# Output product, memory's keys and values, and cross attention: from an order written by hand to one stream placed by durations

## The reference, cut to what matters

```python
x = x + jnp.concatenate([attn_out, mlstm_out], axis=-1) @ w_out[l]
x = x + cross_attention(rmsnorm(x, norm_xattn_g[l]), rmsnorm(mem, norm_mem_g[l]),
                        wq_x[l], wkv_x[l], wo_x[l])
hf = rmsnorm(x, norm_ffn_g[l])          # the feed-forward part follows

def cross_attention(hq, hm, wq, wkv, wo):   # mem has 256 rows; 4 heads of 256
    q = (hq @ wq).reshape(B, S, X_HEADS, X_HEAD_DIM)
    kv = hm @ wkv
    ...
    s = jnp.einsum('bshd,bmhd->bhsm', q, k) * (X_HEAD_DIM ** -0.5)
    a = jax.nn.softmax(s, axis=-1)
    o = jnp.einsum('bhsm,bmhd->bshd', a, v).reshape(B, S, X_HEADS * X_HEAD_DIM)
    return o @ wo
```

## Time and profile before

| | |
|---|---|
| median of 3 runs | 2723.42 us (2719.78 to 2723.84) |
| the profiled execution | 2715.8 us, of which the span from first to last instruction is 2714.0 |
| TensorE busy (matmuls) | 2475.5 us, 91% of the span |
| VectorE, ScalarE busy | 1424.6 us (52%), 942.4 us (35%) |
| mean granted TensorE clock | 0.953 of full speed |
| the stretch that is changed | 500.36 to 926.5 us |

### The profile page before, as it was taken

How to read it: one execution, slowest core, us unless ns; L and a number is a source line. 1 busy time by engine, 2 the same in 40 slices (tenths; PEclk the granted TensorE clock), 3 DMA queues, 4 the chain that set the end, 5 groups by cost and what they waited for, 6 DMA issues and landing times.

```text
span 2714.0 us, 41559 instructions
## 1 busy us (share of the span) xinstructions
PE 2475.5 (91%) x18010; PEld 1991.9 (73%) x18010; DVE 1424.6 (52%) x2500; ACT 942.4 (35%) x1584; POOL 79.6 (3%) x61
## 2 busy tenths in 40 slices
PE   3989988988899999999999998799999999589879
PEld 2777765777778788888888886566777777377757
DVE  4633855565234655534555446653354455666653
ACT  4324542344223333322333324543322232234341
POOL 0000000000000000000000000020000001200000
PEclk9999997989999999999999999888999998699989
DMA  4444310334211333333333333322222311211033
GB/s 144 111 123 123 104 48 1 122 95 131 63 55 52 91 99 94 100 93 101 94 98 96 95 93 107 106 74 87 93 61 66 114 47 35 89 39 39 10 121 120
DMA packets 358335, 233.07 MB, mean 86 GB/s; under 512 B 9604, under 2 KB 332292, under 8 KB 358024
## 3 DMA queue, kind: packets, MB, share of 16 engines
q1 hardware_dynamic: 355416, 224.83, 27.7%
q10 hardware_dynamic: 2736, 5.57, 0.5%
HBM read 211.50 MB, written 18.87 MB: 85 GB/s over the span
## 4 chain that ended last, share of the span: by engine, by line
PE 80%; DVE 11%; ACT 5%; issue 1%; DMA 1%; SPq 0%; DVEq 0%; ACTq 0%
PE PS L1239 19%; PE PS L1240 18%; PE PS L1241 18%; PE PS L1583 4%; PE PS L1225 3%; PE PS L1259 2%; PE PS L1261 2%; PE PS L1260 2%; PE PS L1501 1%; DVE SR L1713 1%; DVE SB L1839 1%; ACT SR L2332 1%; PE PS L1467 1%; PE PS L1431 1%; PE PS L1521 1%
## 5 line engine op out<-in xcount | busy, mean ns | idle before, releaser
L1239 PE MATMUL PS<-SR 128*128 128x512 f32 (+2 forms) x2384 | 959.9, 403 | 57.7 <-DVE SR L1713 40.4
L1240 PE MATMUL PS<-SR 128*128 128x512 f32 (+2 forms) x2384 | 935.5, 392 | 0.0
L1241 PE MATMUL PS<-SR 128*128 128x512 f32 (+2 forms) x2384 | 934.1, 392 | 0.0
L1713 DVE TENSOR_TENSOR SR<-SB,SR 128x1024 fp32r<-128x1024 f32 (+2 forms) x328 | 395.9, 1210 | 467.4 <-ACT SR L2332 467.1
L1239 PEld LDWEIGHTS PS<-SR 128*128 128x128 f32 (+1 forms) x2384 | 455.4, 191 | 182.4 <-DVE SR L1713 43.5
L1241 PEld LDWEIGHTS PS<-SR 128*128 128x128 f32 (+1 forms) x2384 | 455.1, 191 | 96.8
L1240 PEld LDWEIGHTS PS<-SR 128*128 128x128 f32 (+1 forms) x2384 | 456.0, 191 | 89.7 <-issue 2.2
L2332 ACT ACTIVATE SR<-SB 128x1024 fp32r<-128x1024 f32 (+2 forms) x328 | 338.3, 1036 | 295.1 <-DMA SB<-in_w_down 115.0
L1583 PEld LDWEIGHTS PS<-SB 64*64 64x64 f32 x4096 | 129.6, 137 | 41.0 <-issue 21.6
L1583 PE MATMUL PS<-SB 64*64 64x64 f32 x4096 | 142.4, 223 | 11.9 <-DVE SB L2213 5.5
L1225 PE MATMUL PS<-SB 128*128 128x128 f32 (+3 forms) x680 | 103.5, 288 | 41.6 <-DVE SB L2095 14.0
(11 more groups left out here) (238 smaller groups left out, 2502.4 us busy)
## 6 DMA issues: line engine op xcount, KB each, us to landing
SB<-in_w_in SPq DMA_DIRECT2D x110, 512.0 KB, 4.0
SB<-in_w_up SPq DMA_DIRECT2D x88, 512.0 KB, 3.9
SB<-in_w_out SPq DMA_DIRECT2D x32, 512.0 KB, 4.5
SB<-in_w_down SPq DMA_DIRECT2D x32, 512.0 KB, 4.2
SB<-in_w_ada SPq DMA_DIRECT2D x12, 1024.0 KB, 6.7
asides<-SB SPq DMA_DIRECT2D x40, 256.0 KB, 4.4
SB<-in_wkv SPq DMA_DIRECT2D x16, 512.0 KB, 3.8
SB<-in_wq SPq DMA_DIRECT2D x16, 512.0 KB, 4.2
```

Of the source, the lines that this page charges most:

```text
L1239: pe.matmul(out, whi[:, k - k0, :], hi[k], start=(k == 0), stop=False)
L1240: pe.matmul(out, whi[:, k - k0, :], lo[k], start=False, stop=False)
L1241: i = pe.matmul(out, wlo[:, k - k0, :], hi[k], start=False, stop=(k == j.K - 1))
L1713: v.tensor_tensor(m.f32r(a, kn * cn), m.f32(a, kn * cn), m.f32r(a + 1024, kn * cn).bitcast(F32), SUB).then_inc(*on("split.v", p))
```

## The change

The stretch is written by `flow`. `cross` yields its softmax as three steps (`cross_s`, `cross_x`, `cross_p`), waits for room and for the block ahead of it, and two streams take the eight blocks from one list. `mix_parts` becomes `mix_part(h, k)`; those of half 1 are a side stream (`mix_later`). The norms `mem`, `x0`, `x1` and `ffn0` are side streams, each from the point on at which its input is complete. `work` gets durations for the new steps. The pieces of `out0` shrink to four k-blocks, those of `q` and `o` to two. The scaling of the softmax is one instruction with a broadcast operand where it was four. x is read again in two transfers of 2 MB, one for each half, and memory's 1 MB stands between them in SP's queue; `mem_load` is gone. An addition into x waits for its own half alone.

```diff
             dst=lambda t, h=h: m.mo[:, t, hs(h)])
         job(f"out{h}", d["w_out"], 0, 128, 8, m.MX[h], lambda k, h=h: [("mix.v", "lo", h, k)], "add", "gemm.v",
-            cut=4 if h else 8, dst=lambda t, h=h: m.xs[h][t], wait=lambda t: [("x", 7)], half=h)
-        job(f"q{h}", d["wq"], 0, 128, 8, m.H2[h], normed(f"x{h}"), "copy", "gemm.a",
+            cut=4, dst=lambda t, h=h: m.xs[h][t], wait=lambda t, h=h: [(f"xr{h}", 0)], half=h)
+        job(f"q{h}", d["wq"], 0, 128, 8, m.H2[h], normed(f"x{h}"), "copy", "gemm.a", cut=2,
             dst=lambda t, h=h: m.qx[:, t, hs(h)], wait=UP("pe", "kv0"))
         job(f"o{h}", d["wo"], 0, 128, 8, m.H2[h], lambda k, h=h: [("cross.v", "lo", n) for n in range(4 * h, 4 * h + 4)],
-            "add", "gemm.v", dst=lambda t, h=h: m.xs[h][t], half=h,
+            "add", "gemm.v", cut=2, dst=lambda t, h=h: m.xs[h][t], half=h,
             wait=lambda t, h=h: [("gemm.v", "ev", f"out{h}", t)])
         job(f"ug{h}", d["w_up"], 0, 128, 22, m.HB, normed(f"ffn{h}"), "conv_f", "gemm.a", half=h,
             dst=lambda t: m.gf[t], wait=UP("pe", "down0" if h else "o1"))
...
+    if name[:6] == "cross_":
+        return {"cross_s": [("pe", 3.5), ("v", 1.6)], "cross_x": [("a", 2.0)], "cross_p": [("v", 1.6)],
+                "cross_t": [("pe", 0.9), ("a", 0.6), ("v", 0.3)], "cross_o": [("pe", 3.6), ("a", 1.1), ("v", 1.25)]}[name]
+    if name == "mix_part":
+        return [("a", 0.6), ("v", 0.7)]
     if name[:3] == "ml_":
         return {"ml_e": [("pe", 1.7), ("v", 2.8)], "ml_x": [("a", 1.5)], "ml_q": [("pe", 1.7), ("v", 1.4)],
                 "ml_s": [("pe", 1.75), ("v", 1.22)], "ml_k": [("pe", 0.9), ("a", 3.1)], "ml_o": [("pe", 0.9), ("v", 1.22)],
...
     def cross(self, n):
+        if n:
+            yield from self.after(("cs", n - 1))
+        yield from self.after("kv", f"q{n // 4}")
+        yield from self.room((self.pairs, 1), (self.P, 1))
+        self.done.add(("cs", n))
         b, free = self.pairs.take()
         p, pfree = self.P.take()
         st = self.stat()
+        yield [("cross_s", n, b, free, st)]
         self.pairs.give(b, ("cross.a", "x", n))
-        yield [("cross_s", n, b, free, p, pfree, st)]
+        yield [("cross_x", n, b, p, pfree, st)]
+        yield [("cross_p", n, p, st)]
+        if n:
+            yield from self.after(("ct", n - 1))
+        yield from self.room((self.pairs, 1), (self.PT, 1))
+        self.done.add(("ct", n))
         b, free = self.pairs.take()
         self.P.give(p, ("cross.pe", "t", n))
         q, qfree = self.PT.take()
         self.pairs.give(b, ("cross.a", "pt", n), ("cross.v", "pt", n))
         yield [("cross_t", n, b, free, p, q, qfree)]
+        yield from self.room((self.pairs, 1))
         b, free = self.pairs.take()
         self.PT.give(q, ("cross.pe", "o", n))
         self.pairs.give(b, ("cross.v", "lo", n))
-        return [("cross_o", n, b, free, q)]
+        yield [("cross_o", n, b, free, q)]
+        self.done.add(("cross", n))
+
+    def crosses(self, units):
+        while units:
+            yield from self.cross(units.pop(0))
+
+    def mix_later(self):
+        for k in range(0, 8, 2):
+            yield [("mix_part", 1, k), ("mix_part", 1, k + 1)]
+        self.done.add("parts")
+        yield [("mark", "parts")]
+
+    def memory(self):
+
+        yield from self.gemmT("kx")
+        for c in range(2):
+            yield from self.gemmN(f"vx{c}")
+        yield [("mark", "kv")]
+        kv = ("upto", "pe", "kv")
+        for i in range(2):
+            self.P.give(i, kv)
+            self.PT.give(i, kv)
+        self.done.add("kv")
 
     def ffn(self, half):
         for t in range(23):
@@ -1162,27 +1202,17 @@
                   self.gates(), self.gate_logs(), self.ada(), self.rms("mix1", self.room), *[self.windows(units) for _ in range(3)], self.attended(),
                   self.mlstm(0, 2), self.mlstm(1, 3))
         self.mark("ml")
-        self.emit(("x_again",), ("mix_parts", 0), ("mix_parts", 1))
-        self.mark("parts")
-        self.run(T("out0"))
-        self.emit(("mem_load",))
-        self.together(T("out1"), chain(self.rms("mem"), self.rms("x0")))
-        self.mark("kv0")
-        self.together(chain(T("kx"), N("vx0"), N("vx1")), self.rms("x1"))
-        self.mark("kv")
-        self.run(T("q0"))
-        self.mark("q0")
-        kv = ("upto", "pe", "kv")
+        self.emit(("x_again",), *[("mix_part", 0, k) for k in range(8)])
         self.P, self.PT = Places([]), Places([])
-        for i in range(2):
-            self.P.give(i, kv)
-            self.PT.give(i, kv)
-        self.together(T("q1"), staggered([self.cross(n) for n in range(4)], 2), 2)
-        self.mark("q1")
-        self.together(T("o0"), staggered([self.cross(n) for n in range(4, 8)], 2), 2)
-        self.mark("o0")
-        self.together(T("o1"), self.rms("ffn0"))
-        self.mark("o1")
+        units = list(range(8))
+        crossed = lambda h: self.after(*[("cross", n) for n in range(4 * h, 4 * h + 4)])
+        self.flow(chain(T("out0"), self.after("parts"), T("out1"), self.flagged("kv0", ("mark", "kv0")), self.after("mem"),
+                        self.memory(), self.after("x0"), T("q0"), self.flagged("q0", ("mark", "q0")), self.after("x1"), T("q1"),
+                        self.flagged("q1", ("mark", "q1")), crossed(0), T("o0"), self.flagged("o0", ("mark", "o0")), crossed(1),
+                        T("o1"), self.flagged("o1", ("mark", "o1"))),
+                  self.mix_later(), *[self.crosses(units) for _ in range(2)], self.rms("mem", self.room),
+                  chain(self.after("out0", "parts"), self.rms("x0", self.room)), chain(self.after("kv0"), self.rms("x1", self.room)),
+                  chain(self.after("o0"), self.rms("ffn0", self.room)))
         self.conv = 0
         self.run(self.ffn(0))
...
-    def mix_parts(h):
+    def mix_part(h, k):
         hi, lo = m.MX[h][0:2]
-        for k in range(8):
-            w.wait_ge(*at("mix.a", "hi", h, k))
-            v.tensor_tensor(lo[k], m.mixs[k][:, 512 * h:512 * h + 512], hi[k].bitcast(F32), SUB).then_inc(
-                *on("mix.v", "lo", h, k))
-
-    def cross_s(n, b, free, p, pfree, st):
-        P, s = v3(m.Pv2[p], 4), v3(pair(b), 4)
-        mx, nm, sm, _ = stats(st, 4)
+        w.wait_ge(*at("mix.a", "hi", h, k))
+        v.tensor_tensor(lo[k], m.mixs[k][:, 512 * h:512 * h + 512], hi[k].bitcast(F32), SUB).then_inc(*on("mix.v", "lo", h, k))
+
+    def cross_s(n, b, free, st):
+        mx, nm, _, _ = stats(st, 4)
         w.wait_ge(*at("cross.pe", "s", n))
-        for e in S.each(pfree):
-            w.wait_ge(*e)
-        v.tensor_reduce(mx, s, AX.X, MAX).then_inc(*on("cross.v", "max", n))
+        v.tensor_reduce(mx, v3(pair(b), 4), AX.X, MAX).then_inc(*on("cross.v", "max", n))
         w.wait_ge(*at("cross.v", "max", n))
         v.tensor_scalar(nm, mx, -1.0 / 16, None, MUL).then_inc(*on("cross.v", "neg", n))
+
+    def cross_p(n, p, st):
+        P, sm = v3(m.Pv2[p], 4), stats(st, 4)[2]
         w.wait_ge(*at("cross.a", "x", n))
         v.reciprocal(sm, sm).then_inc(*on("cross.v", "rcp", n))
         w.wait_ge(*at("cross.v", "rcp", n))
-        for g in range(4):
-            i = v.tensor_scalar(P[:, g, :], P[:, g, :], sm[:, g:g + 1], None, MUL)
-        i.then_inc(*on("cross.v", "p", n))
+        v.tensor_tensor(P, P, sm.unsqueeze(2).to_broadcast([128, 4, 256]), MUL).then_inc(*on("cross.v", "p", n))
 
     def cross_t(n, b, free, p, q, qfree):
...
 
-    def mix_parts(h):
+    def mix_part(h, k):
         for e in ("pe", "v", "a"):
             for x in S.upto(e, "ml"):
                 w.wait_ge(*x)
-        for k in range(8):
-            a.activation(m.MX[h][0][k], m.mixs[k][:, 512 * h:512 * h + 512], ACT.Copy).then_inc(*on("mix.a", "hi", h, k))
-
-    def cross_s(n, b, free, p, pfree, st):
+        a.activation(m.MX[h][0][k], m.mixs[k][:, 512 * h:512 * h + 512], ACT.Copy).then_inc(*on("mix.a", "hi", h, k))
+
+    def cross_x(n, b, p, pfree, st):
         P, s = v3(m.Pv2[p], 4), v3(pair(b), 4)
         mx, nm, sm, _ = stats(st, 4)
         w.wait_ge(*at("cross.v", "neg", n))
+        for e in S.each(pfree):
+            w.wait_ge(*e)
         for g in range(4):
             i = a.activation(P[:, g, :], s[:, g, :], ACT.Exp, bias=nm[:, g:g + 1], scale=1.0 / 16, accum_out=sm[:, g:g + 1])
...
         mlstm_done()
-        for k in range(8):
-            sp.dma_start(m.XT[:, k, :], d["xT"][k * 128:(k + 1) * 128, :]).then_inc(*on("x", k, by=16))
-
-    def mem_load():
-        mlstm_done()
-        sp.dma_start(v3(m.work(28672, 2048), 8), d["memT"].rearrange("(k p) n -> p k n", p=128)).then_inc(
-            *on("mem", 0, by=16))
+        for h in range(2):
+            sp.dma_start(m.XT[:, :, 512 * h:512 * h + 512],
+                         d["xT"][:, 512 * h:512 * h + 512].rearrange("(k p) n -> p k n", p=128)).then_inc(*on(f"xr{h}", 0, by=16))
+            if not h:
```

(2 more changed lines are left out.)

10 lines of the change are left out of this document (5 added, 5 removed).

## The result

The changed kernel takes **2681.08 us** (median of four runs, 2676.67 to 2685.52) against 2721.60 for the kernel before beside it (2719.35 to 2723.84, four runs). The ratio is 0.9857, 95% interval 0.984 to 0.9875: 1.4% faster. The forecast was 2685. The profiled execution took 2676.67 (span 2674.8).

What follows compares the result with a forecast made beforehand. TensorE's waits and low clock from `out0` to `o1` were taken as the bound. Of 55.7 us lost, 17.5 would stay (5.9, 6.0, 5.6, 0), so 38.2 less: 2685 us, range 2675 to 2696.

Steps and rivals of the forecast that it cites:

- the 55.7 us that the change can give: TensorE's loss against full-clock work: 54.1 us from `out0` to `o1` plus 1.6 behind; the most the change can give.
- A: `out0` and `out1`: 5.9 of 11.3 us lost stays, as 1.4 cold start, 3.5 memory's transfer, 1.0 norm wait.
- Memory's transfer: Early `out0`: memory lands late, its squares delay a split, TensorE waits 2.6 us plus 0.9 of clock, 3.5 new.
- The norm `x0`: Moves into `out1`: sum 9.4 us behind the end of `out0`, waiting 1.0; its outputs lie under `out1`.
- B: Memory's keys and values (`kx`, `vx0`, `vx1`): 6.0 of 18.9 us lost stays, VectorE still the tightest of the stretch.
- C: `q0` to `o1` with cross attention: 5.6 of 23.9 us stays, 2.9 scaled from planned sliding-window stretch 208 to 388, 2.7 unnamed.
- The scaling: Cross attention's softmax: one instruction for four adds 0.8 us on VectorE over eight blocks, hidden under TensorE's work.
- Behind the stretch: First feed-forward tile after `o1`: its 1.6 us wait goes, leaving 0; the order of what follows is untouched.
- B did not keep its loss: Rival for memory's keys and values: VectorE can't follow the 2.86 us tiles, 12.9 of gain goes, 2698 us; chance 0.14.
- no transpose waited: Slower rival in cross attention: each of eight transposes meets its softmax unfinished, 65 us lost there, 2745 us; chance 0.04.
- Memory's norm did not block the front: Rival in `out0`: memory's squares, additions and sum hold the engines 11 to 14 us, not 3.5; 2694 us; chance 0.12.
- waits only change place: Rival over the stretch: TensorE stands at side steps instead, 50 of 55.7 us stay, 2718 us or more; chance 0.04.

Runs made afterwards that it cites:

- one_step: The kernel before, with one side step for each tile of `q1` and `o0` where there were two: 2697.85 us, ratio 0.9929 to the kernel before.
- whole_tiles: The changed kernel without the cut of `q` and `o` tiles into two pieces: 2691.84 us, ratio 0.9895 to the kernel before.
- prompt: The changed kernel with the planner booking nothing for weight splits in the stretch, so norms come promptly: 2680.96 us, ratio 0.9869 to the kernel before.
- outs: The changed kernel with a norm's output step booked on VectorE alone in the stretch: 2675.31 us, ratio 0.9832 to the kernel before.
- stream_c: The changed kernel with everything ahead of `q0` in the old hand order, new transfers kept: 2702.58 us, ratio 0.9943 to the kernel before.

## Why the prediction was right, step by step

- **What bounds it, and the 55.7 us that the change can give.** Right. The stretch got 39.1 us shorter and the median fell by 40.5, where 38.2 was forecast.
- **A, 5.9.** Measured 4.5, by other terms. The cold start, 1.4, is 3.0 in this execution, since the clock stays longer at the 1.2 GHz level. That is not the change: one_step has the order of the kernel before up to here, whole_tiles that of the changed kernel, and each start comes with both. The first 8 us of `out0`, in before and one_step, then in changed and whole_tiles (8 x (1 - 0.82) = 1.4 lost, 8 x (1 - 0.62) = 3.0):

```profile
500.36:508.36 8.00, 8.00 (x29) 6.54 (x30) 8.00 (x14) 7.89 (x15) 0.00 (x0) 0.82 0.92 330
497.15:505.15 8.00, 8.00 (x23) 6.32 (x24) 8.00 (x14) 7.88 (x15) 0.00 (x0) 0.62 0.95 347
```

```profile
497.54:505.54 8.00, 8.00 (x23) 6.32 (x24) 5.26 (x9) 3.81 (x8) 0.00 (x0) 0.62 0.99 346
497.65:505.65 8.00, 8.00 (x29) 6.54 (x30) 5.27 (x9) 3.82 (x8) 0.00 (x0) 0.82 0.99 347
```

  In all four TensorE waits 3.4 us just ahead. What decides between the two starts, these runs don't show.

- **Memory's transfer, 3.5.** The mechanism was right: the squares are the longest wait of ScalarE there, the split follows them, and TensorE waits at the third tile. The measured 1.28, with no clock lost, is smaller by the luck of the long start. Memory landed as forecast: the squares began 11.6 us behind the issue of x's first transfer at 496.41 (I had 11.2). But TensorE wanted the tile 1.7 us later, since it had run at the low clock for longer. In whole_tiles, with the same order and the short start that the prediction had assumed, the wait is 2.66 (I had 2.6), the clock reads 0.89 from 505 to 520, and A loses 6.1. The changed kernel, then whole_tiles:

```profile
507.99 2.57 ACT L2418 ACTIVATE SB<-SB 128x256 f32<-128x256 f32 x8 [6.64 <-DMA SB<-in_memT]
...
512.82 0.50 PE L1269 MATMUL PS<-SR 128*128 128x512 f32 x1 [1.28 <-DVE SR L1743]
```

```profile
512.83 0.50 PE L1269 MATMUL PS<-SR 128*128 128x512 f32 x1 [2.66 <-DVE SR L1743]
```

- **The norm `x0`, 1.0 of wait, sum 9.4 us behind `out0`, outputs under `out1`.** The failed step. The planner's table was read, and not that its running times only go forward; the sum came some 30 us later. That is why nothing waits for it. And the assumed placement would have cost more than its 1.0: in prompt that wait was 0.8, but memory's sum waited 3.3 us more and lowered the clock, for which the sum of A had nothing.
- **B, 6.0.** Mis-sized at 0.9 for the same reason. For the placement that it assumed the size was good: prompt lost 7.2. The reason was half right. The step of reciprocal and two outputs does make a split late (1.9 us in prompt, 2.8 in outs); the other wait comes from the squares in ScalarE's queue (2.2 in prompt, 1.1 in the changed kernel), which the prediction didn't count. VectorE's load was no bound: it is busy 29.8 us of 46.2.
- **C, 5.6.** Mis-sized at 9.4. The row of 208 to 388 was the right neighbour for the blocks themselves (forecast 2.9; stream_c and prompt lose 0.6 and 0.4), and there the 2.7 without a name went too. In one_step 3.0 without a name remain. What I left out is `x1`'s norm reaching into the first two blocks: 4.3 idle (3.60 and 0.72) and 3.0 at the low clock in the second scores. The rest, 2.1, has no row that I can name.
- **The scaling, 0.8 under cover.** Right: 1.22 against 1.14 a block, and no difference in time. The prediction says that by the figures of the Trainium skill, "VectorE: DVE Perf Modes", the sum is the same 0.8. That was reckoned wrong: four times 128 + 150 cycles against 1,024 + 150, at the page's 0.96 GHz, differ by 0.06 us a block, an estimate of 0.5 for the eight. That rate and fixed cost nearly cancel, the rows bear out.
- **Behind the stretch, 0.** Right for the feed-forward's first tile (4.47 busy of 4.47). That the order of what follows isn't touched was wrong for the second layer, and gave 4 to 6 us of waits back.
- **The rivals.** B did not keep its loss, and no transpose waited. Memory's norm did not block the front here, but in prompt, where its sum stands closer, A lost 11.6, twice the forecast; the mechanism by which waits only change place happened once, at 3.6 us.

The forecast of the total was near in part by luck: two errors of one cause, B by 5.1 too high and C by 3.8 too low, nearly cancel. The mechanism in the main was right, since the waits on the norm's additions and on the softmax's scaling are gone and none took their place but the one at 692. The smaller pieces of `out0` and the later parts of the mix were not tested by themselves.

## What to carry to other kernels

When steps are placed by a planner, work its clock through by hand before you cost a stage: an engine's running time that never goes back over a gap drifts ahead when two kinds of step book the same two engines in opposite order, and the drift both spreads side work (here good: it took the long steps of a norm out of the short tiles) and pushes it into the next stage (bad where it holds a buffer there). Look for the longest single step in each queue that the product's own inputs share, before you look at an engine's load. The planner's state at the end of a rebuilt stretch is an input to all that is planned behind it; compare the order of untouched parts too. And try the pace of the old order first: one side step a tile in place of two gave half of the whole gain.
